# Squares of x and their sums behind the four leading weight pieces, the norm's row sum behind the third output tile

## What is computed

```
def rms_norm(x, g):
    y = xf * lax.rsqrt(jnp.mean(xf * xf, axis=-1, keepdims=True) + EPS)
    return (y * g.astype(jnp.float32)).astype(x.dtype)

def macaron_half(x, g, w_in, w_out):
    a, b = jnp.split(rms_norm(x, g) @ w_in, 2, axis=-1)
    return x + 0.5 * ((jax.nn.silu(a) * b) @ w_out)
```

## Time and profile before

| | |
|---|---|
| median of 3 runs | 1364.91 us (1364.26 to 1365.6) |
| the profiled execution, its own time | 1362.81 us |
| its span, first to last instruction | 1361.0 us |
| busy: PE, DVE, ACT, POOL | 95%, 55%, 41%, 13% |
| mean granted clock of TensorE | 0.985 |

### The profile page before, as it was taken

How to read it: one execution, slowest core, us unless ns; L and a number is a source line. 1 busy time by engine, 2 the same in 40 slices (tenths; PEclk the granted TensorE clock), 3 DMA queues, 4 the chain that set the end, 5 groups by cost and what they waited for, 6 DMA issues and landing times.

```text
span 1361.0 us, 22014 instructions
## 1 busy us (share of the span) xinstructions
PE 1298.8 (95%) x8593; PEld 1263.7 (93%) x8593; DVE 752.6 (55%) x1152; ACT 563.8 (41%) x799; POOL 178.1 (13%) x202
## 2 busy tenths in 40 slices
PE   6999999999898999999999989999995999999999
PEld 6999999998787999999999989999983789999998
DVE  6756565444655655554455565554445746565532
ACT  6534354353354544333354343433344535333322
POOL 3200020054013100000040000001061420000000
PEclk9999999999999999999999999999997999999999
DMA  7454454553220444443454324444441014444343
GB/s 256 148 152 152 152 164 135 197 186 124 93 90 2 154 155 154 154 167 128 151 183 153 124 96 152 154 146 148 160 156 55 6 63 155 154 147 140 128 149 123
DMA packets 39210, 187.41 MB, mean 138 GB/s; under 512 B 4304, under 2 KB 14288, under 8 KB 23920
## 3 DMA queue, kind: packets, MB, share of 16 engines
q1 hardware_dynamic: 37824, 183.38, 39.2%
q0 software_dynamic: 1184, 3.13, 1.0%
q10 hardware_dynamic: 144, 0.11, 0.0%
HBM read 179.70 MB, written 6.90 MB: 137 GB/s over the span
## 4 chain that ended last, share of the span: by engine, by line
PE 88%; DVE 6%; ACT 2%; issue 1%; POOL 1%; DMA 1%; SPq 0%; ACTq 0%; DVEq 0%
PE bank L453 26%; PE bank L454 25%; PE bank L455 25%; PE bank L744 1%; PE bank L626 1%; PE bank L745 1%; PE bank L746 1%; ACT whi L881 1%; DVE wlo L1180 1%; DVE qz L1220 1%; PE bank L653 1%; POOL ew L1659 1%; PE bank L656 1%; PE outs L678 1%; DMA raw<-in_w_ffn_out 1%
## 5 line engine op out<-in xcount | busy, mean ns | idle before, releaser
L453 PE MATMUL bank<-xhi,whi 128*128 128x320 f32 (+1 forms) x1760 | 550.4, 313 | 16.1 <-DVE wlo L1457 10.5
L455 PE MATMUL bank<-xhi,wlo 128*128 128x320 f32 (+1 forms) x1760 | 546.8, 311 | 0.0
L454 PE MATMUL bank<-xlo,whi 128*128 128x320 f32 (+1 forms) x1760 | 546.7, 311 | 0.0
L1180 DVE TENSOR_TENSOR wlo<-raw,whi 128x2048 fp32r<-128x2048 f32 (+1 forms) x183 | 377.8, 2064 | 249.1 <-ACT whi L881 249.0
L881 ACT ACTIVATE whi<-raw 128x2048 fp32r<-128x2048 f32 (+1 forms) x183 | 315.5, 1724 | 257.7 <-PE bank L455 249.2
L453 PEld LDWEIGHTS bank<-xhi,whi 128*128 128x128 f32 x1760 | 333.9, 190 | 20.4 <-issue 14.4
L454 PEld LDWEIGHTS bank<-xlo,whi 128*128 128x128 f32 x1760 | 334.0, 190 | 0.6 <-issue 0.2
L455 PEld LDWEIGHTS bank<-xhi,wlo 128*128 128x128 f32 x1760 | 333.8, 190 | 0.0
L453 PE MATMUL bank<-hhi,whi 128*128 128x320 f32 x704 | 219.3, 312 | 3.2 <-DVE wlo L1180 1.7
L455 PE MATMUL bank<-hhi,wlo 128*128 128x320 f32 x704 | 217.5, 309 | 0.0
L454 PE MATMUL bank<-hlo,whi 128*128 128x320 f32 x704 | 217.5, 309 | 0.0
(11 more groups left out here) (203 smaller groups left out, 1114.2 us busy)
## 6 DMA issues: line engine op xcount, KB each, us to landing
raw<-in_w_ffn_in SPq DMA_DIRECT2D x87, 1024.0 KB, 4.7
raw<-in_w_ffn_out SPq DMA_DIRECT2D x64, 704.0 KB, 4.1
raw<-in_w_in_a SPq DMA_DIRECT2D x10, 1024.0 KB, 4.7
raw<-in_w_out SPq DMA_DIRECT2D x8, 1024.0 KB, 4.7
raw<-in_w_kv SPq DMA_DIRECT2D x6, 1024.0 KB, 4.7
raw<-in_w_mkv SPq DMA_DIRECT2D x4, 1024.0 KB, 4.8
raw<-in_w_in_b SPq DMA_DIRECT2D x4, 1024.0 KB, 4.7
x<-in_xT SPq DMA_DIRECT2D x4, 320.0 KB, 5.0
```

The lines of the kernel that those rows point to most:

```text
L453: mm(acc, wh, mhi(ks[q]), start=start and q == 0, stop=False)
L454: mm(acc, wh, mlo(ks[q]), start=False, stop=False)
L455: last = mm(acc, wl, mhi(ks[q]), start=False, stop=stop and q == nk - 1)
L1180: tt(wlo[slot][:, 0:size], raw[slot][:, 0:size], f32(whi[slot][:, 0:size]), ALU.subtract).then_inc(lo_ready[slot], 1)
```

## The change

ACT no longer squares within the loop over the quarters. It squares slices 0 to 3 behind slot 1's `whi`, then makes slot 0's `whi` of the second pair (which `ffn_in` did before, behind the norm's root), and then squares slices 4 to 7. PE's matmul for the norm stands behind the third tile (j = 2) in `in0`, not behind the first. DVE subtracts slot 0's `wlo` of the second pair ahead of the norm's Newton step, not behind it. POOL's and SP's programs are the same.

```
--- before.py
+++ after.py
@@ -548,7 +548,7 @@
                         product(banks[j][:, 0:R], slot, col, 256, range(KD), KD,
                                 lambda k: xhi[:, k, :], lambda k: xlo[:, k, :], True, True, each
                                 ).then_inc(acc_ready, 1)
-                        if first and j == 0 and stage in NORM:
+                        if first and j == (2 if stage == "in0" else 0) and stage in NORM:
                             row_norm(stage, R)
                         if after:
                             after(j)
@@ -951,8 +951,6 @@
                 m0 = {"in0": 0, "in1": KF, "in2": 2 * KF, "in3": 3 * KF}[stage]
                 if stage in NORM:
                     row_norm(stage, R)
-                if stage == "in0":
-                    split_hi(0, n0 + 1, BLK, acc_ready, t0 + 2)
                 nc.scalar.preload_act_table_set("silu_and_others")
 
                 def body(i, size):
@@ -1092,9 +1090,12 @@
                 act.wait_ge(d_piece[q] if q < 3 else landed[0], 16)
                 nc.scalar.activation(whi[0][:, 512 * q:512 * (q + 1)], raw[0][:, 512 * q:512 * (q + 1)], ACT.Copy
                                      ).then_inc(piece_hi if q < 3 else hi_ready[0], 1)
-                for k in (2 * q, 2 * q + 1):
-                    stream_square(NORM["in0"], k, x[:, k, :], R)
             split_hi(1, 0, BLK, None, 0)
+            for k in range(4):
+                stream_square(NORM["in0"], k, x[:, k, :], R)
+            split_hi(0, PAIR0["in0"] + 1, BLK, acc_ready, TILE0["in0"] + 2)
+            for k in range(4, KD):
+                stream_square(NORM["in0"], k, x[:, k, :], R)
 
             def memory_in(i):
                 if i == 0:
@@ -1265,10 +1266,10 @@
             def ffn_in(stage, after=None):
                 n0, t0 = PAIR0[stage], TILE0[stage]
                 m0 = {"in0": 0, "in1": KF, "in2": 2 * KF, "in3": 3 * KF}[stage]
+                if stage == "in0":
+                    split_lo(0, n0 + 1, BLK)
                 if stage in NORM:
                     row_norm(stage, R)
-                if stage == "in0":
-                    split_lo(0, n0 + 1, BLK)
 
                 def body(i, size):
                     for c in range(2):
```

## The result

The changed kernel takes 1367.3 us (median of 12 runs, 1365.12 to 1369.56), the kernel before 1364.47 on the same chip (12 runs): ratio 1.0022, 95% interval 1.0013 to 1.0031, or **+3.0 us** by the ratio (+1.8 to +4.2). In a second comparison on another occasion it was 1367.2 to 1363.7, ratio 1.0027 (1.0017 to 1.0038). The profiled execution took 1368.55, its span is 1366.7.

The account below looks back on a forecast made before the run. PE bounds the kernel, holding 88% of the chain; the start of tile 4 is the yardstick. Bias matmul at 33.8 plus 0.74 gives 34.6 against 31.66, +2.9 us: 1367.8 against the median, range 1365.2 to 1370.9.

Parts of the forecast that it names:

- Squares out of the loop: Tile 0: without squares in the quarter loop, its last quarter starts at 12.4 instead of 16.37, 4.0 us earlier.
- The hold and the last add: POOL's sums: DVE instructions hold its copy and square 4's add; the last add ends at 27.1, before at 15.3.
- DVE's swap: DVE's lo half ahead of Newton's steps costs nothing, since the norm now comes after it in any case.
- The wait ahead of the norm: Behind tile 2: PE reaches the norm's matmul at 21.4 to 24, idles 3 to 5.7 us until 27.1.
- The clock: PE's idle time brings the low clock level; norm ends at 28.2, tile 3 at 33.2, against 31.2 without the fall.
- The constants: POOL's loads behind the sums: last issued at 29.4, landing 4.3 later at 33.7; the bias matmul starts at 33.8.
- Adds not held: Rival, chance 0.15: sums end at 24.2, tile 4 moves -0.8 to +1.6 us, giving 1364.1 to 1366.5.
- The norm not in the way: Rival, chance 0.07: sums ready by about 22.3, PE not stopped behind tile 2; tile 4 at 28.1, 3.6 earlier, 1361.3.
- Late constants with a second fall: Rival, chance 0.13: PE waits 2 us between tile 3 and bias matmul, clock falls again; up to +6.3, 1369.5 to 1371.2.

Follow-up runs that it names:

- PE kept busy: Changed kernel plus 36 useless matmuls into an unused PSUM bank between tile 2 and the norm: 1368.08 and 1367.33 us, ratios 1.0037 and 1.0025 to the kernel before.
- all squares first: Changed kernel with all eight squares ahead of slot 0's hi copy of the second pair on ACT: 1365.04 us, ratio 1.0010 to the kernel before.
- best kernel: Changed kernel with squares 0 to 2 ahead of slot 1's hi copy and POOL's constant loads issued behind add 2: 1361.45 and 1361.23 us.
- three squares in the gap: Changed kernel with squares 0 to 2 in ACT's idle time ahead of slot 1's hi copy, 3 to 7 behind it: 1366.03 us, ratio 1.0023.
- the norm behind tile 3: Changed kernel with the norm's matmuls one tile later still, behind tile 3: 1370.13 us, ratio 1.0042 to the kernel before.
- the norm alone: Kernel before with one edit, the norm's matmuls behind the third tile: 1368.14 us, ratio 1.0030 to the kernel before.

## Why the prediction was right, step by step

*Result.* 1367.8 forecast, 1367.3 measured; +2.9 forecast, +3.0 and +3.7 measured; tile 4 forecast at 34.6, profiled at 36.0 and 34.8. The mechanism held (held adds, PE's wait, the low level behind it). That the sum agrees to 0.1 us is luck: the interval is +1.8 to +4.2, the two profiles are 1.3 us apart at tile 4, and several terms were off, as follows.

*Squares out of the loop: right in kind, 0.4 to 1.5 us too large.* xlo is at 0.5, the quarters at 0.69. Tile 0's last quarter started at 13.86 in the first profile and at 12.76 in the second, not at 12.4: ACT waited for landings (in the first profile for the quarters of the weights at 7.88 and 10.62, and for the slices of x). The slowest quarter took 8.0 us to land in the first and 6.7 in the second, where I took the 6.5 of the kernel before. The gain was 2.5 and 3.6 us, and it was lost like the rest.

*The hold and the last add: right.* 27.1 forecast; 27.3 in the second profile, whose copy starts at 15.72 (forecast 15.7), and 28.6 in the first, where slot 1's block landed 1.2 us later. The first profile's extra delay is a landing (ACT's hi copy at 14.64, I took 13.3).

*DVE's swap "costs nothing": wrong.* With the old order back the sums ended 1.7 us sooner. The hold itself stood in the sum for the last add, but I did not see that the swap makes it: with the old order DVE is idle while POOL adds. My reason, that the norm comes after in any case, looked only at DVE's own path.

*The wait ahead of the norm: right.* 3 to 5.7 forecast, 5.24 and 5.25 measured, and 2.6 with the squares rearranged. (Tile 2's earliest end is 21.0 by the forecast's own terms, 17.5 + 3.5, not 21.4; it ended at 23.4 and 22.1.)

*The clock: right, a little longer than taken.* It fell in the wait, and from the norm's start to the bias matmul it was 6.7 us in both profiles (28.63 to 35.31, 27.36 to 34.03), where I had 6.1 to the end of tile 3. The run with PE kept busy shows that the idle time causes it, since the level stayed and the same stretch took 5.4 to 5.5, 1.1 to 1.2 of them waiting. That an idle time of some size is always followed by the low level is not shown: with all squares first PE idled 2.60 and then 1.95 us, and the level stayed.

*The constants: right that their cover goes, wrong that they are last.* I let them end the sum at 33.7. They landed at 30.82 + 3.3 = 34.1 and 29.55 + 3.6 = 33.2, 1.2 and 0.9 ahead of PE. Landing was faster than my 4.3, and tile 3 later than my 33.2. In the second profile the two errors cancel within 0.3 us (bias matmul at 34.03, forecast 33.8); in the first it came 1.5 later, nearly all of it the later landing of slot 1's block. As soon as anything else is improved they are the wait: 1.95, 1.1 to 1.2, 3.35 and 4.65 us in four of the kernels above.

*Rivals.* Adds not held: excluded by the copy's 2.21, against 0.61 with DVE idle. The norm not in the way: excluded by the 5.24. The best kernel, though, has tile 4 at 28.15 and 27.76, where that rival's sum had 28.1. Late constants with a second fall: not in the changed kernel, but a wait for the last constant with a low stretch behind it is what happened in the second profile with PE kept busy, with three squares in the gap and, the level falling within the wait, with the norm behind tile 3.

*What stays open.* The share of low stretches behind tile 4 differs between executions of one program by more than the effect (3.6 us between two profiles of the kernel before). With 5 to 12 runs each, medians are good to about 1.4 us (0.1%); the runs with PE kept busy, with three squares in the gap, with the norm alone and with the norm behind tile 3 were 1 to 3 us above what their tile 4 and first low stretch say, and I can't tell whether that is chance.

## What to carry over

An instruction that is moved off one critical path becomes late for its other users: follow each result of it (here the sums, the norm, then the constants queued behind the sums on POOL) to who waits for it last. Where two engines hold each other up, look for the time in which one of them is idle or has work that is not held (here POOL's DMA issues), and let the other's long instruction fall there. PE idle times of a few us can cost twice, once as wait and once as the low level behind it. A kernel may also be judged wrongly by one profile: look first where the profiled execution lies among the others.

## What the runs showed of the hardware

POOL's DMA issues (0.75, 0.57, 0.56, 0.53, 0.60) took the same time while DVE ran an instruction with two SBUF inputs, from 15.65 to 17.9, as with DVE idle (28.5 to 31.4 in the changed kernel), while a copy or an add waits for such an instruction's end (a copy 2.21 against 0.61, four adds 5.61 against 3.87). The Trainium skill, SBUF — State Buffer, section Who interferes with whom, says that such a DVE instruction contends with GpSimd instructions that read SBUF and not with those that only write it, and gives for descriptor generation that it needs the write side (as inferred); the rows agree.

Two executions of the same program, 0.06 us apart at tile 4, ended 3.6 us apart. They differ in which idle times of PE are followed by 3.4 us or more granted at 0.50.

The last constant, 128 KB issued by POOL, landed 3.3 and 3.6 us after its issue in the two profiles of the changed kernel, 4.0 with all squares first, 4.4 in the first profile of the best kernel, 5.4 with three squares in the gap and 6.0 in the kernel before.
